# A fused transformer kernel on one core: the norms between its stages and the start of its down projections rewritten

## The chip, the cores and the metric

The kernel runs on one core of a Trainium2 chip. The core has a matmul engine (TensorE, PE in the profile; PEld are its weight loads), VectorE (DVE), ScalarE (ACT), GpSimd (POOL) and the queue engine SyncE (SP) that issues most DMAs. Each engine has its own instruction stream; they meet only at semaphores. The metric is the device time of one execution in microseconds (us), lower being better.

## The reference

One call computes a block with a gated recurrent mixer and a long convolution, and then two more layers. In order:

```python
# first block
u = rms_norm(x, mix_pre_g) * (1 + sc1) + sh1          # sh, sc, g come from cond @ ada_w
h, y = mlstm(u), conv_branch(u)
mix = concat([h, y]) @ w_out
x = x + g1 * rms_norm(mix, mix_post_g)
u = rms_norm(x, ffn_pre_g) * (1 + sc2) + sh2
a, gt = split(causal_dwconv(u @ ffn_up))
x = x + g2 * rms_norm((silu(gt) * a) @ ffn_down, ffn_post_g)
# two layers, mixer = attention with forget gates, then a gated linear recurrence
x = x + rmsnorm(mixer(rmsnorm(x, gain0)), gain1)
x = x + rmsnorm(swiglu_ffn(rmsnorm(x, gain2)), gain3)
```

x is 512 positions by 1024 channels, the feed-forward width is 2816, everything is float32.

## The kernel before

**Layout.** Activations lie channel-major: a tensor of 1024 channels is 8 tiles (KT = 8) of 128 partitions by 512 positions (T). x, m (the output of the last projection), u_hi and u_lo (the next stage's input, split into a rounded float32r part and the rest) live in SBUF. There are eight PSUM banks, ps[0] to ps[7], of 128x512 float32.

**Matmuls.** Each float32 product is three float32r matmuls of 512 columns (hi by hi, lo by hi, hi by lo), all recorded at line 308 (gemm_chunk), 332 (gemm_first) or 488 (the mixers' outputs). Weights stream from HBM in chunks of 128x1024. SP loads chunk c + 4 into the slot of chunk c once c has been used; POOL rounds it (w_hi, line 812) and takes the rest (w_lo, line 818); then PE may use it. That order is fixed: POOL goes through the chunks in the stream's order, with the sums of the norms (below) put in between.

**Up and down.** Each feed-forward stage makes 22 pairs of up chunks (FT = 22). The gate and the product of pair j are made by DVE and ACT into f_hi and f_lo, with banks 2s and 2s+1 for s = j % 2. Then out_pe makes the 8 output tiles of the down projection, each of three chunks of 8, 7 and 7 k-tiles, in banks 0 and 1 in turn. Before output tile n it waits for the copy of tile n - 2:

```python
pe.wait_ge(og.act.sem, og.act.at("copy", og_body * it + s - 2))
```

For the first two tiles there is no such copy: the semaphore has a credit of two turns, which og.act.open(act) adds. In the kernel before, that call is the first statement of out_act on ACT's stream, behind the last gate of the up stage. out_act then squares each output tile into sq and copies it into m, and DVE adds the squares into acc.

**Norms.** There are seven: n0 before the first mixer (no output tile before it), n1 before the first feed-forward stage ("shift", with a modulation), n2 to n5 ("late"), n6 at the end (only the residual). For each but n0: PE sums acc and the last square over the channels (line 345, 347), ACT takes Ln and Exp (lines 369, 371) to get 1/rms in ps[5], DVE makes t = m * gain / rms (line 431) and x = x + t (line 435), tile by tile. norm_act begins with an ACT table load (line 374).

In a late norm the next projection does not wait for the second rms: per tile ACT makes u_hi = x * gain (line 381) and the square (384), DVE makes u_lo (424), and gemm_first starts with tile 0 of three chunks at once. POOL adds up the squares (413, 416), late_sum_pe sums them over the channels behind gemm_first (359), and the projection's results are scaled by this second 1/rms (the tile rms) afterwards. While it waits for the first u_lo, PE runs six filler matmuls (keep_busy, line 339).

**Modulation.** The adaptive modulation columns are made in four turns of DVE partial products (ada_dve_pieces) and PE column sums (ada_pe, line 636) during the first mixer's output projection.

Of the kernel before, what the change touches and what calls it, by code (L numbers as in the profile page):

```python
# [18 lines left out]
P = 128  # L19
T = 512  # L20
D = 1024
KT = D // P
# [6 lines left out]
FT = 2816 // P  # L29
# [71 lines left out]
def build(nc, xT, wstream, ada, params, outT, rows1, rows2):  # L101
# [150 lines left out]
    class Norm:  # L252
# [3 lines left out]
        def __init__(self, name, post, pre):  # L256
            self.post, self.pre = post, pre
            if post:
# [3 lines left out]
                for n in range(KT):  # L262
                    order += [f"t{n}"] + ([f"lo{n - 1}"] if n and pre == "late" else []) + [f"x{n}"]
                self.vx = Steps(ctx, nc, name + "_dvex", order + ([f"lo{KT - 1}"] if pre == "late" else []))
# [7 lines left out]
            if pre == "late":  # L272
                self.ahq = Steps(ctx, nc, name + "_acthisq", [f"{w}{n}" for n in range(KT) for w in ("hi", "sq")])
# [4 lines left out]
    norms = [Norm(f"n{i}", i > 0, pre) for i, pre in enumerate(("shift", "shift", "late", "late", "late", "late", None))]  # L278
# [6 lines left out]
    outs = [OutGemm(f"og{i}") for i in range(6)]  # L285

# [49 lines left out]
    def keep_busy(pe, count):  # L336

        for _ in range(count):
            nc.tensor.matmul(ps[2][:], mean_w[:], levels[:, 0:4, :].bitcast(f32), start=True, stop=True)

    def norm_pe(pe, N, og):
        if N.post:
# [4 lines left out]
            N.pe1.did(nc.tensor.matmul(ps[5][:], mean_w[:], sq[(KT - 1) % 2][:], start=False, stop=True), "sum")  # L347
            if N.pre == "late":
                keep_busy(pe, 6)
        if N.pre == "shift":  # L350
# [3 lines left out]
            keep_busy(pe, 3)  # L354
# [18 lines left out]
    def norm_act(act, N, gain, shift):  # L373
        act.preload_act_table_set(LN_EXP)  # L374
# [3 lines left out]
        if N.pre == "late":  # L378
            for n in range(KT):
                act.wait_ge(N.vx.sem, N.vx.at(f"x{n}"))  # L380
                N.ahq.did(nc.scalar.activation(u_hi[:, n, :], x[:, n, :], ACT.Identity, scale=gain(n)), f"hi{n}")  # L381
                if n >= 2:
                    act.wait_ge(N.pq.sem, N.pq.at(f"add{max(n - 2, 1)}"))
                N.ahq.did(nc.scalar.activation(sq[n % 2][:], x[:, n, :], ACT.Square), f"sq{n}")
# [22 lines left out]
    def norm_pool(pool, N):  # L407

        if N.pre == "late":
# [9 lines left out]
    def norm_dve(dve, N, post_gain, gain, shift, wait_cols=None):  # L419

        def low_late(n):

            dve.wait_ge(N.ahq.sem, N.ahq.at(f"hi{n}"))
            N.vx.did(nc.vector.scalar_tensor_tensor(u_lo[:, n, :], x[:, n, :], gain(n), u_hi[:, n, :].bitcast(f32),  # L424
                                                    ALU.mult, ALU.subtract), f"lo{n}")

        if N.post:
            dve.wait_ge(N.a1.sem, N.a1.at("rstd"))
            for n in range(KT):
                t = ps[4 + 2 * (n % 2)]  # L430
# [1816 lines left out]
```

## Time and profile before

| | before |
|---|---|
| median of 3 runs | 2395.82 us (2394.5 to 2397.46) |
| the profiled execution's own time | 2394.99 us |
| its span, first to last instruction | 2393.2 us |
| PE busy | 2273.7 us, 95% |
| POOL busy | 1478.8 us, 62% |
| DVE busy | 1163.8 us, 49% |
| ACT busy | 629.0 us, 26% |
| mean granted TensorE clock | 0.979 |

Busy time says how long instructions of an engine were under way. A matmul is recorded as longer than its share of the engine, since matmuls overlap, so the distance between the starts of two of them is the measure of their pace.

### The profile page before, as it was taken

Reading aid. Unit: us, or ns where it says so; the run is one execution under the profiler, and the core shown is the slowest. Engines: PE = TensorE matmul, PEld = TensorE weight load, DVE = VectorE, ACT = ScalarE, POOL = GpSimd, SP = SyncE. Lnnn points to the kernel's source line nnn. Section 1 sums busy time; section 2 is a strip of 40 time slices with the busy share of each in tenths; the row PEclk is TensorE's granted clock in tenths of the full one; section 3 lists DMA queues with packets and bytes.
Section 4 is the critical chain, followed back from the end, with each engine's and each line's share of the span. In section 5 each row is a group of like instructions: output and inputs, shape, how many; then the busy total and the mean of one; then the engine's idle time right before and its main releaser. Section 6 shows DMA issues by size and latency. Waiting matters only on the chain. (4 is left out here: it accounts for less than half of the span.)

```text
span 2393.2 us, 28178 instructions
## 1 busy us (share of the span) xinstructions
PE 2273.7 (95%) x9952; PEld 1768.8 (74%) x9952; DVE 1163.8 (49%) x1942; ACT 629.0 (26%) x1077; POOL 1478.8 (62%) x704
## 2 busy tenths in 40 slices
PE   7999999999999998999899999998898979999997
PEld 4777776767887876777678887876777767888785
DVE  4878877974433007555342221027778755322112
ACT  2322325132222013333331111023444433111100
POOL 3756763648777886444288777884222228877784
PEclk9999999999999999999999999999999989999999
DMA  5322323722222331222122322321111112222232
GB/s 217 106 80 71 96 88 106 288 76 93 96 96 80 105 104 63 71 71 71 53 74 93 96 93 91 105 79 62 53 53 53 60 37 80 90 94 96 88 105 79
DMA packets 56503, 216.35 MB, mean 90 GB/s; under 512 B 6232, under 2 KB 6232, under 8 KB 53232
## 3 DMA queue, kind: packets, MB, share of 16 engines
q1 hardware_dynamic: 52992, 206.96, 25.9%
q10 hardware_dynamic: 3440, 8.44, 1.0%
q8 instruction: 45, 0.74, 0.1%
q14 instruction: 26, 0.21, 0.0%
HBM read 213.23 MB, written 2.15 MB: 90 GB/s over the span
## 5 line engine op out<-in xcount | busy, mean ns | idle before, releaser
L812 POOL TENSOR_TENSOR w_hi<-raw,ones 128x1024 fp32r<-128x1024 f32 x315 | 603.0, 1914 | 628.8 <-DMA raw<-in_wstream 627.7
L818 POOL TENSOR_TENSOR w_lo<-raw,w_hi 128x1024 fp32r<-128x1024 f32 x342 | 837.3, 2448 | 230.7 <-ACT w_hi L1521 206.0
L308 PE MATMUL ps<-u_hi,w_hi 128*128 128x512 f32 x1760 | 719.2, 409 | 13.1 <-DVE hv L1974 6.2
L308 PE MATMUL ps<-u_lo,w_hi 128*128 128x512 f32 x1760 | 699.3, 397 | 0.0
L308 PE MATMUL ps<-u_hi,w_lo 128*128 128x512 f32 x1760 | 698.5, 397 | 0.0
L308 PEld LDWEIGHTS ps<-u_hi,w_hi 128*128 128x128 f32 x1760 | 334.1, 190 | 92.1 <-issue 7.7
L308 PEld LDWEIGHTS ps<-u_hi,w_lo 128*128 128x128 f32 x1760 | 332.6, 189 | 81.4
L308 PEld LDWEIGHTS ps<-u_lo,w_hi 128*128 128x128 f32 x1760 | 333.7, 190 | 75.9 <-issue 3.1
L308 PE MATMUL ps<-f_hi,w_hi 128*128 128x512 f32 x528 | 210.5, 399 | 7.7 <-ACTq L85 7.7
L308 PE MATMUL ps<-f_hi,w_lo 128*128 128x512 f32 x528 | 210.1, 398 | 0.0
L308 PE MATMUL ps<-f_lo,w_hi 128*128 128x512 f32 x528 | 210.0, 398 | 0.0
L1668 DVE SCALAR_TENSOR_TENSOR y<-ps,prm,y 128x511 f32<-128x511 f32 (+14 forms) x240 | 176.1, 734 | 11.0 <-ACT y L1266 3.4
L529 DVE TENSOR_TENSOR acc<-acc,sq 128x512 f32<-128x512 f32 x30 | 39.8, 1326 | 253.0 <-ACT sq L519 252.8
L519 ACT ACTIVATE sq<-ps 128x512 f32<-128x512 f32 x48 | 28.7, 599 | 472.0 <-PE ps L308 350.7
L1934 DVE TENSOR_TENSOR ps<-ps,rms 128x512 f32<-128x512 f32 x44 | 30.7, 698 | 194.0 <-PE ps L308 194.0
L308 PEld LDWEIGHTS ps<-f_hi,w_hi 128*128 128x128 f32 x528 | 100.0, 189 | 33.2 <-issue 5.0
L308 PEld LDWEIGHTS ps<-f_hi,w_lo 128*128 128x128 f32 x528 | 99.9, 189 | 24.7
L308 PEld LDWEIGHTS ps<-f_lo,w_hi 128*128 128x128 f32 x528 | 100.0, 189 | 24.4
L1143 PE MATMUL ps<-hl 128*128 128x128 f32 x448 | 63.9, 288 | 30.3 <-DVE hl L2049 25.9
L1143 PEld LDWEIGHTS ps<-hl 128*128 128x128 f32 x448 | 61.2, 201 | 39.2 <-DVE hl L2049 30.2
L1484 ACT ACTIVATE f_hi<-fraw 128x512 f32 x44 | 27.8, 632 | 210.3 <-DVE fraw L1939 210.3
L1932 DVE TENSOR_TENSOR ps<-ps,rms 128x512 f32<-128x512 f32 x44 | 30.7, 698 | 94.0 <-PE ps L308 84.3
(305 smaller groups left out, 2928.5 us busy)
## 6 DMA issues: line engine op xcount, KB each, us to landing
raw<-in_wstream SPq DMA_DIRECT2D x342, 512.0 KB, 3.4
ada_buf<-in_ada SPq DMA_DIRECT2D x16, 1024.0 KB, 5.8
ada_start<-in_ada SPq DMA_DIRECT2D x8, 1024.0 KB, 16.7
cbc<-decay_rows ACTq DMA_DIRECT2D x8, 512.0 KB, 3.7
x<-in_xT SPq DMA_DIRECT2D x1, 2048.0 KB, 7.6
bc<-gate_rows ACTq DMA_DIRECT2D x4, 512.0 KB, 4.9
out_T<-x ACTq DMA_DIRECT2D x8, 256.0 KB, 2.0
prm<-in_params SPq DMA_DIRECT2D x1, 357.5 KB, 3.0
```

The source lines that it names most:

```text
L308: last = nc.tensor.matmul(out, a, b, start=(start and k == 0 and i == 0), stop=(stop and k == nk - 1 and i == 2))
L519: og.act.did(nc.scalar.activation(sq[n % 2][:], ps[n % banks][:], ACT.Square), "sq")
L529: ins = nc.vector.tensor_tensor(acc[:], acc[:], sq[n % 2][:], ALU.add)
L812: g.tensor_tensor(w_hi[slot][:], raw[slot][:], ones[:, 0:1].to_broadcast([P, D]), ALU.mult).then_inc(chunk_hi, 1)
L818: g.tensor_tensor(w_lo[slot][:], raw[slot][:], w_hi[slot][:].bitcast(f32), ALU.subtract).then_inc(chunk_split, 1)
L1143: last = nc.tensor.matmul(ps[b][:, ts], (hk if src is None else src)[:, ts], (hq if src is None else src)[:, ts], start=True, stop=True)
L1484: aS.did(A(f_hi[:, bass.ds(j, 1), :], fraw[s][:, 0:T], ACT.Identity), "hi")
L1668: v_cv[i].did(V.scalar_tensor_tensor(y[:, 2 * h + i, back:], ps[4 + i][:, 0:T - back], head_col(h, HP_CVW + CV_TAPS * i + j), y[:, 2 * h + ...
L1932: vS.did(V.tensor_tensor(ps[2 * s][:], ps[2 * s][:], rms[:], ALU.mult), "sg")
L1934: vS.did(V.tensor_tensor(ps[2 * s + 1][:], ps[2 * s + 1][:], rms[:], ALU.mult), "sa")
```

## The change

1. The credit of all six output projections is given at the very start of ACT's stream (open_outs). In place of the old wait, ffn_pe waits before the down projection for step "f" of pair FT - 2, the last pair that used banks 0 and 1.
2. The ACT table load for Ln and Exp moves from the start of norm_act to the start of out_act.
3. In n1, the last turn of the modulation is summed on PE behind the norm's own sum, into bank 3, and its columns are made on DVE behind the residual.
4. In n2 to n5, t and the new x are made in a PSUM bank out of three (4, 6 and 2 or 3). u_hi, u_lo and the square read it there, and ACT copies x back to SBUF: three ACT passes a tile instead of two. t of tile n waits for the square of tile n - 3. The filler matmuls write bank 7.
5. In n6, t of even tiles is made in place in m, and POOL adds it to x; DVE does the odd tiles as before.

```diff
--- before.py
+++ after.py
@@ -253,14 +253,17 @@
-        def __init__(self, name, post, pre):
-            self.post, self.pre = post, pre
+        def __init__(self, name, post, pre, spare):
+            self.post, self.pre, self.banks = post, pre, (4, 6, spare)
             if post:
                 self.pe1 = Steps(ctx, nc, name + "_pe1", ["sum"])
                 self.a1 = Steps(ctx, nc, name + "_act1", ["ln", "rstd"])
                 order = []
                 for n in range(KT):
                     order += [f"t{n}"] + ([f"lo{n - 1}"] if n and pre == "late" else []) + [f"x{n}"]
+                if pre is None:
+                    order = [step for n in range(KT) for step in ([f"t{n}", f"x{n}"] if n % 2 else [f"t{n}"])]
+                    self.px = Steps(ctx, nc, name + "_poolx", [f"x{n}" for n in range(0, KT, 2)])
                 self.vx = Steps(ctx, nc, name + "_dvex", order + ([f"lo{KT - 1}"] if pre == "late" else []))
             if pre == "shift":
                 self.asq = Steps(ctx, nc, name + "_actsq", ["sq"])
@@ -270,12 +273,17 @@
                 self.ah = Steps(ctx, nc, name + "_acthi", ["hi"])
                 self.vl = Steps(ctx, nc, name + "_dvelo", ["lo"])
             if pre == "late":
-                self.ahq = Steps(ctx, nc, name + "_acthisq", [f"{w}{n}" for n in range(KT) for w in ("hi", "sq")])
+                self.ahq = Steps(ctx, nc, name + "_acthisq", [step for n in range(KT + 1) for step in
+                                                        ([f"hi{n}"] if n < KT else []) + ([f"x{n - 1}", f"sq{n - 1}"] if n else [])])
                 self.pq = Steps(ctx, nc, name + "_poolsq", [f"add{n}" for n in range(1, KT)])
                 self.pe2 = Steps(ctx, nc, name + "_pe2", ["sum"])
                 self.a2 = Steps(ctx, nc, name + "_act2", ["ln", "rstd"])
-    norms = [Norm(f"n{i}", i > 0, pre) for i, pre in enumerate(("shift", "shift", "late", "late", "late", "late", None))]
+        def new(self, n):
+            return ps[self.banks[n % 3]]
+    norms = [Norm(f"n{i}", i > 0, pre, 2 if i == 2 else 3) for i, pre in enumerate(("shift", "shift", "late", "late", "late", "late", None))]
     class OutGemm:
         def __init__(self, name):
@@ -283,6 +291,10 @@
             self.dve = Steps(ctx, nc, name + "_dve", [f"acc{n}" for n in range(1, KT - 1)])
     outs = [OutGemm(f"og{i}") for i in range(6)]
+    def open_outs(act):
+        for og in outs:
+            og.act.open(act)
     def matmuls(out, pairs, n_inc=None, start=True, stop=True):
@@ -333,25 +345,27 @@
                 if k == KT - 1:
                     last.then_inc(gemm_done, 1)
-    def keep_busy(pe, count):
+    def keep_busy(pe, count, bank):
         for _ in range(count):
-            nc.tensor.matmul(ps[2][:], mean_w[:], levels[:, 0:4, :].bitcast(f32), start=True, stop=True)
-
-    def norm_pe(pe, N, og):
+            nc.tensor.matmul(ps[bank][:], mean_w[:], levels[:, 0:4, :].bitcast(f32), start=True, stop=True)
+    def norm_pe(pe, N, og, between=None):
         if N.post:
             pe.wait_ge(og.dve.sem, og.dve.at(f"acc{KT - 2}"))
             nc.tensor.matmul(ps[5][:], mean_w[:], acc[:], start=True, stop=False)
             pe.wait_ge(og.act.sem, og.act.at("sq", KT - 1))
             N.pe1.did(nc.tensor.matmul(ps[5][:], mean_w[:], sq[(KT - 1) % 2][:], start=False, stop=True), "sum")
+            if between:
+                between()
             if N.pre == "late":
-                keep_busy(pe, 6)
+                keep_busy(pe, 6, 7)
         if N.pre == "shift":
             for n in range(KT):
                 pe.wait_ge(N.asq.sem, N.asq.at("sq", n))
                 N.pe2.did(nc.tensor.matmul(ps[7][:], mean_w[:], sq[n % 2][:], start=(n == 0), stop=(n == KT - 1)), "sum")
-            keep_busy(pe, 3)
+            keep_busy(pe, 3, 2)
     def late_sum_pe(pe, N):
@@ -371,17 +385,26 @@
         S.did(nc.scalar.activation(out[:], out[:], ACT.Exp, scale=-0.5), "rstd")
     def norm_act(act, N, gain, shift):
-        act.preload_act_table_set(LN_EXP)
+        if not N.post:
+            act.preload_act_table_set(LN_EXP)
+        def late_home(n):
+            act.wait_ge(N.vx.sem, N.vx.at(f"lo{n}"))
+            N.ahq.did(nc.scalar.activation(x[:, n, :], N.new(n)[:], ACT.Identity), f"x{n}")
+            if n >= 2:
+                act.wait_ge(N.pq.sem, N.pq.at(f"add{max(n - 2, 1)}"))
+            N.ahq.did(nc.scalar.activation(sq[n % 2][:], N.new(n)[:], ACT.Square), f"sq{n}")
         if N.post:
             act.wait_ge(N.pe1.sem, N.pe1.at("sum"))
             inverse_root(act, N.a1, ps[5], ps[5], 1)
         if N.pre == "late":
             for n in range(KT):
                 act.wait_ge(N.vx.sem, N.vx.at(f"x{n}"))
-                N.ahq.did(nc.scalar.activation(u_hi[:, n, :], x[:, n, :], ACT.Identity, scale=gain(n)), f"hi{n}")
-                if n >= 2:
-                    act.wait_ge(N.pq.sem, N.pq.at(f"add{max(n - 2, 1)}"))
-                N.ahq.did(nc.scalar.activation(sq[n % 2][:], x[:, n, :], ACT.Square), f"sq{n}")
+                N.ahq.did(nc.scalar.activation(u_hi[:, n, :], N.new(n)[:], ACT.Identity, scale=gain(n)), f"hi{n}")
+                if n:
+                    late_home(n - 1)
+            late_home(KT - 1)
             act.wait_ge(N.pe2.sem, N.pe2.at("sum"))
             inverse_root(act, N.a2, rms, ps[7], 1)
         if N.pre == "shift":
@@ -406,6 +429,10 @@
     def norm_pool(pool, N):
+        if N.pre is None:
+            for n in range(0, KT, 2):
+                pool.wait_ge(N.vx.sem, N.vx.at(f"t{n}"))
+                N.px.did(nc.gpsimd.tensor_tensor(x[:, n, :], x[:, n, :], m[:, n, :], ALU.add), f"x{n}")
         if N.pre == "late":
             for n in range(1, KT):
                 pool.wait_ge(N.ahq.sem, N.ahq.at(f"sq{n}"))
@@ -418,21 +445,28 @@
     def norm_dve(dve, N, post_gain, gain, shift, wait_cols=None):
         def low_late(n):
             dve.wait_ge(N.ahq.sem, N.ahq.at(f"hi{n}"))
-            N.vx.did(nc.vector.scalar_tensor_tensor(u_lo[:, n, :], x[:, n, :], gain(n), u_hi[:, n, :].bitcast(f32),
-                                                    ALU.mult, ALU.subtract), f"lo{n}")
+            N.vx.did(nc.vector.scalar_tensor_tensor(u_lo[:, n, :], N.new(n)[:], gain(n),
+                                                    u_hi[:, n, :].bitcast(f32), ALU.mult, ALU.subtract), f"lo{n}")
         if N.post:
             dve.wait_ge(N.a1.sem, N.a1.at("rstd"))
             for n in range(KT):
-                t = ps[4 + 2 * (n % 2)]
-                N.vx.did(nc.vector.scalar_tensor_tensor(t[:], m[:, n, :], post_gain(n), ps[5][:], ALU.mult, ALU.mult), f"t{n}")
+                t = N.new(n)[:] if N.pre == "late" else ps[4 + 2 * ((n if N.pre else n // 2) % 2)][:]
+                if N.pre is None and n % 2 == 0:
+                    t = m[:, n, :]
+                if N.pre == "late" and n >= 3:
+                    dve.wait_ge(N.ahq.sem, N.ahq.at(f"sq{n - 3}"))
+                N.vx.did(nc.vector.scalar_tensor_tensor(t, m[:, n, :], post_gain(n), ps[5][:], ALU.mult, ALU.mult), f"t{n}")
                 if n and N.pre == "late":
                     low_late(n - 1)
+                if N.pre is None and n % 2 == 0:
+                    continue
                 dve.wait_ge(N.vx.sem, N.vx.at(f"t{n}"))
-                N.vx.did(nc.vector.tensor_tensor(x[:, n, :], x[:, n, :], t[:], ALU.add), f"x{n}")
+                N.vx.did(nc.vector.tensor_tensor(t if N.pre == "late" else x[:, n, :], x[:, n, :], t, ALU.add), f"x{n}")
             if N.pre == "late":
                 low_late(KT - 1)
         if N.pre == "shift":
@@ -511,7 +545,7 @@
     def out_act(act, og, base, ks, banks=2, done=None):
         nch = len(ks)
-        og.act.open(act)
+        act.preload_act_table_set(LN_EXP)
         for n in range(KT):
             act.wait_ge(gemm_done, done(n) if done else base + (n + 1) * nch)
             if n >= 2:
@@ -618,10 +652,12 @@
     ada_link = Steps(ctx, nc, "ada_link", [f"l{s}{k}" for s in range(ADA_BODY) for k in range(KT - 1)])
+    ADA_BANK = (6, 6, 6, 3)
     def ada_dve_mod(dve, turn):
         dve.wait_ge(p_ada.sem, p_ada.at("sums", turn))
         n = ADA_BODY * ADA_COLS // P
-        v_mod.did(nc.vector.tensor_tensor(mod[:, 2 * KT + n * turn:2 * KT + n * (turn + 1)], ps[6][:, 0:n],
+        v_mod.did(nc.vector.tensor_tensor(mod[:, 2 * KT + n * turn:2 * KT + n * (turn + 1)], ps[ADA_BANK[turn]][:, 0:n],
                                           prm[:, COL["ada_b"] + 2 * KT + n * turn:COL["ada_b"] + 2 * KT + n * (turn + 1)],
                                           ALU.add), "mod")
@@ -988,7 +1024,7 @@
             pe.wait_ge(outs[0].act.sem, outs[0].act.at("copy", n - GROUP))
             wout_pe(n, 0, range(KT))
             wout_pe(n, 1, range(KT))
-            turn = {3: 0, 5: 1, 6: 2, 7: 3}.get(n)
+            turn = {3: 0, 5: 1, 6: 2}.get(n)
             if turn is not None:
                 ada_pe(pe, turn)
@@ -1012,10 +1048,11 @@
                     for j in range(2):
                         pair(it, s, j)
             S, step = prev
+            pe.wait_ge(S.sem, S.at("f", FT - 2))
             out_pe(pe, og, dbase, DOWN_K, lambda k: f_hi[:, k, :], lambda k: f_lo[:, k, :],
                    ready=lambda k: pe.wait_ge(S.sem, S.at(step, k)))
-        norm_pe(pe, norms[1], outs[0])
+        norm_pe(pe, norms[1], outs[0], lambda: ada_pe(pe, 3))
         ffn_pe(norms[1], C_UP1, C_DOWN1, {"g": (v_ff1, "g0"), "a": (v_ff1, "a0")}, outs[1], (v_ff1, "lo"))
         norm_pe(pe, norms[2], outs[1])
@@ -1229,6 +1266,7 @@
     @block.scalar
     def _(act):
         A = nc.scalar.activation
+        open_outs(act)
         act.wait_ge(prm_landed, 16)
         a_set.did(A(cvec[:], prm[:, COL["c"]:COL["c"] + KT], ACT.Sigmoid), "sig_c")
         act.wait_ge(const_ready, 14)
@@ -1595,7 +1633,8 @@
         out_act(act, outs[5], C_DOWN3, DOWN_K)
         norm_act(act, norms[6], None, None)
         for n in range(KT):
-            act.wait_ge(norms[6].vx.sem, norms[6].vx.at(f"x{n}"))
+            S = norms[6].vx if n % 2 else norms[6].px
+            act.wait_ge(S.sem, S.at(f"x{n}"))
             act.dma_start(outT[:, n, :], x[:, n, :]).then_inc(out_landed, 16)
         act.wait_ge(out_landed, 16 * KT)
@@ -1780,18 +1819,27 @@
             for n in (2 * it, 2 * it + 1):
                 if 1 <= n < KT - 1:
                     out_sum_dve(dve, outs[0], n)
-        ada_dve_mod(dve, KT // 2 - 1)
-        dve.wait_ge(v_mod.sem, v_mod.at("mod", KT // 2 - 1))
-        for name, o, src, gain in (("g1", 8, 16, "mix_post"), ("a2", 16, 32, "ffn_pre"), ("g2", 24, 40, "ffn_post")):
...
-        dve.wait_ge(v_col.sem, v_col.at("g2"))
+        def modulation_columns(names):
+            for name, o, src, gain in (("g1", 8, 16, "mix_post"), ("a2", 16, 32, "ffn_pre"), ("g2", 24, 40, "ffn_post")):
+                if name in names:
...
+            dve.wait_ge(v_col.sem, v_col.at(names[-1]))
+        def last_columns():
+            ada_dve_mod(dve, KT // 2 - 1)
+            dve.wait_ge(v_mod.sem, v_mod.at("mod", KT // 2 - 1))
+            modulation_columns(["g2"])
+        dve.wait_ge(v_mod.sem, v_mod.at("mod", KT // 2 - 2))
+        modulation_columns(["g1", "a2"])
         norm_dve(dve, norms[1], lambda n: col_a[:, 8 + n:9 + n], lambda n: col_a[:, 16 + n:17 + n],
-                 lambda n: mod[:, 24 + n:25 + n])
+                 lambda n: mod[:, 24 + n:25 + n], last_columns)
         v_ff1.open(dve)
```

## Rows read from the trace of the kernel before

**Rows 1.** The page, part 1: busy time, share of span, instructions of each engine.
```profile
PE 2273.7 (95%) x9952; PEld 1768.8 (74%) x9952; DVE 1163.8 (49%) x1942; ACT 629.0 (26%) x1077; POOL 1478.8 (62%) x704
```

**Rows 2.** Waits of PE, whole span: total us, times, longest us.
```profile
PE ps L308 <- ACTq L85: 7.7, 3, 3.4
```

**Rows 3.** Timeline of PE at two down projections: start us, us, instruction.
```profile
768.80 0.77 PE L308 MATMUL ps<-f_hi,w_hi 128*128 128x512 f32 x1 [3.44 <-ACTq L85]
...
774.06 0.44 PE L308 MATMUL ps<-f_hi,w_hi 128*128 128x512 f32 x1
...
2248.33 0.39 PE L308 MATMUL ps<-u_hi,w_lo 128*128 128x512 f32 x1
2250.83 0.47 PE L308 MATMUL ps<-f_hi,w_hi 128*128 128x512 f32 x1 [2.11 <-ACTq L85]
```

**Rows 4.** Windows: PE, PEld, DVE, ACT, POOL busy (count), PEclk, DMA.
```profile
2250.80:2256.00 5.20, 5.17 (x16) 4.13 (x17) 0.69 (x1) 0.25 (x1) 3.92 (x3) 0.67 0.16 66
...
2250.00:2376.00 126.00, 125.17 (x529) 100.40 (x530) 11.67 (x8) 8.41 (x16) 92.63 (x43) 0.99 0.27 87
```

**Rows 5.** Timeline of the start of n1.
```profile
495.38 1.84 PE L636 MATMUL ps<-ones,ada_acc 128*128 128x1 f32 x16
...
499.08 0.66 ACT L369 ACTIVATE ps<-ps,eps_col 128x512 f32<-128x512 f32 x1 [1.12 <-PE ps L347]
```

**Rows 6.** Timeline of n6, all engines.
```profile
2375.63 1.02 PE L345 MATMUL ps<-acc,mean_w 128*128 128x512 f32 x2
...
2376.49 1.12 PE L347 MATMUL ps<-sq,mean_w 128*128 128x512 f32 x2
2376.93 1.28 ACT L374 ACT_TABLE_LOAD   x1
...
2379.54 0.76 DVE L431 SCALAR_TENSOR_TENSOR ps<-m,prm,ps 128x512 f32<-128x512 f32 x1 [15.65 <-ACT ps L371]
...
2381.05 0.37 ACTq L1599 DMA_DIRECT2D out_T<-x  x1
...
2390.04 0.69 DVE L435 TENSOR_TENSOR x<-x,ps 128x512 f32<-128x512 f32 x1
```

**Rows 7.** Timeline of n5, a late norm, all engines.
```profile
1994.25 5.31 PE L339 MATMUL ps<-levels,mean_w 128*128 128x512 f32 x12
...
1996.34 0.76 DVE L431 SCALAR_TENSOR_TENSOR ps<-m,prm,ps 128x512 f32<-128x512 f32 x1 [7.70 <-ACT ps L371]
...
1999.70 0.47 PE L332 MATMUL ps<-u_hi,w_hi 128*128 128x512 f32 x1
...
2013.01 0.68 DVE L435 TENSOR_TENSOR x<-x,ps 128x512 f32<-128x512 f32 x1
...
2015.05 1.33 POOL L416 TENSOR_TENSOR acc<-acc,sq 128x512 f32<-128x512 f32 x1 [0.82 <-ACT sq L384]
...
2017.49 1.02 PE L359 MATMUL ps<-acc,mean_w 128*128 128x512 f32 x2
...
2024.45 0.50 PE L308 MATMUL ps<-u_hi,w_hi 128*128 128x512 f32 x1 [0.34 <-POOL w_lo L818]
```

**Rows 8.** Timeline of n2, the late norm behind the first down projection.
```profile
898.39 0.76 DVE L431 SCALAR_TENSOR_TENSOR ps<-m,col_a,ps 128x512 f32<-128x512 f32 x1 [17.77 <-ACT ps L371]
...
920.42 1.02 PE L359 MATMUL ps<-acc,mean_w 128*128 128x512 f32 x2
```

**Rows 9.** Lines: count, ns min/median/max, first to last start.
```profile
L405 ACT ACTIVATE u_hi<-ps,mod x16: 687/687/691, 43.8 to 525.1; 128x512 fp32r<-128x512 f32 x16
...
L520 ACT ACTIVATE m<-ps x48: 590/592/620, 420.2 to 2376.3; 128x512 f32<-128x512 f32 x48
...
L424 DVE SCALAR_TENSOR_TENSOR u_lo<-x,prm,u_hi x32: 750/752/2497, 900.7 to 2014.5; 128x512 fp32r<-128x512 f32 x32
...
L435 DVE TENSOR_TENSOR x<-x,ps x48: 673/682/687, 501.2 to 2390.0; 128x512 f32<-128x512 f32 x48
```

**Rows 10.** One line of the last mixer's recurrence, columns as in rows 9.
```profile
L2083 DVE TENSOR_TENSOR hqd<-hq,he x8: 675/2882/2901, 1665.7 to 1942.4; 128x512 f32<-128x512 f32 x8
```

More of the change, by code:

```diff
@@ L635, in ada_pe @@
                 j = s * (ADA_COLS // P) + h
-                last = nc.tensor.matmul(ps[6][:, j:j + 1], ada_acc[:, 4 * (turn % 2) + s, h * P:(h + 1) * P], ones[:, 0:1],
+                last = nc.tensor.matmul(ps[ADA_BANK[turn]][:, j:j + 1], ada_acc[:, 4 * (turn % 2) + s, h * P:(h + 1) * P], ones[:, 0:1],
                                         start=True, stop=True)
@@ L1782, in _ @@
                     out_sum_dve(dve, outs[0], n)
-        ada_dve_mod(dve, KT // 2 - 1)
-        dve.wait_ge(v_mod.sem, v_mod.at("mod", KT // 2 - 1))
-        for name, o, src, gain in (("g1", 8, 16, "mix_post"), ("a2", 16, 32, "ffn_pre"), ("g2", 24, 40, "ffn_post")):
-            g_ = prm[:, COL[gain]:COL[gain] + KT]
-            if name == "a2":
-                ins = V.scalar_tensor_tensor(col_a[:, o:o + KT], mod[:, src:src + KT], 1.0, g_, ALU.add, ALU.mult)
-            else:
-                ins = V.tensor_tensor(col_a[:, o:o + KT], mod[:, src:src + KT], g_, ALU.mult)
-            v_col.did(ins, name)
-        dve.wait_ge(v_col.sem, v_col.at("g2"))
+        def modulation_columns(names):
+            for name, o, src, gain in (("g1", 8, 16, "mix_post"), ("a2", 16, 32, "ffn_pre"), ("g2", 24, 40, "ffn_post")):
+                if name in names:
+                    g_ = prm[:, COL[gain]:COL[gain] + KT]
+                    if name == "a2":
+                        ins = V.scalar_tensor_tensor(col_a[:, o:o + KT], mod[:, src:src + KT], 1.0, g_, ALU.add, ALU.mult)
+                    else:
+                        ins = V.tensor_tensor(col_a[:, o:o + KT], mod[:, src:src + KT], g_, ALU.mult)
+                    v_col.did(ins, name)
+            dve.wait_ge(v_col.sem, v_col.at(names[-1]))
[5 more added lines that the diff above has]
+        modulation_columns(["g1", "a2"])
         norm_dve(dve, norms[1], lambda n: col_a[:, 8 + n:9 + n], lambda n: col_a[:, 16 + n:17 + n],
-                 lambda n: mod[:, 24 + n:25 + n])
+                 lambda n: mod[:, 24 + n:25 + n], last_columns)
         v_ff1.open(dve)
```

## The prediction

> **What bounds the kernel now.** The page's first part comes first: PE is busy for 95% of the span, the other engines for 62% at most [rows 1]. So PE is the bound, and a change gains where it removes time in which PE waits or runs slowly, or shortens the end behind its last matmul. The pace of PE at full clock is one matmul in 0.233 us (two starts in a row in the timeline, such as 2375.63 less the start before it). I then looked for PE's waits. One is met at all three down projections: together 7.7 us, put down to ACT's queue [rows 2]. The timelines show it as a hole between the last up matmul and the first down matmul, and behind it matmuls at a wider distance [rows 3]; a window gives the granted clock there, 0.67 [rows 4]. The rest of PE's idle time lies mostly in the norms, so I read one late norm in order of time [rows 7], another for the difference [rows 8], and the last one [rows 6].
>
> **The credits given at the start.** The last up matmul of the third feed-forward stage starts at 2248.33, the first down matmul at 2250.83; at full pace it would follow after 0.23, so 2.27 us are lost. The profile's idle of 2.11 is this less 0.16, since it counts from the modelled end. For three holes: 7.7 + 3 x 0.16 = 8.2 us [rows 2, 3]. What PE would then wait for is old: step "f" of pair 20 comes two chunks, some 11 us, before. The last gate's own tile is wanted 21 k-tiles on, 63 x 0.233 = 14.7 us later, and it follows the last up matmul by about 3 us. Weights: POOL is busy for 92.6 of 126 us in the down stage [rows 4], and PE waits for nothing else there.
>
> The hole costs more than itself. At 768.80 the matmuls start at wide distances until 774.06: 12 matmuls in 5.26 us, at full pace 2.80, so 2.46 us more. Behind the third hole there are 16 matmuls in 5.2 us at a granted clock of 0.67, where 3.73 would do: 1.47 more [rows 3, 4]. These stretches are at the lower of TensorE's two levels, 1.2 GHz, and follow a PE that stood still. With no hole I take both to go. Bounds: 0 (the slow stretch comes anyway) to 3.9 us. I take 3.9, as PE runs at full clock up to each hole. **Sum: 8.2 + 3.9 = 12.1 us.**
>
> **The table load.** In n6 the norm's sum ends at 2376.49 + 1.12 = 2377.61 but Ln starts only behind the table load, 2376.93 + 1.28 = 2378.21. Ln moves forward to 2377.65, by 0.57, in n2 to n6 [rows 6]. In its new place the load lies in ACT's wait for the first output tile. The Trainium skill ("ScalarE: Activation LUTs", What ACT_TABLE_LOAD costs) gives 1283 ns and a further 1380 ns of drain for a switch to another set. The trace has only the 1.28; by the page each norm would give 1.4 more, 8 us in all, and the rows leave no room for it.
>
> **n1.** Here the column sums of the modulation stand ahead: 495.38 is where the norm's first sum would start. In n6 Ln could start 2377.65 - 2375.63 = 2.02 behind that point; here it starts at 499.08 instead of 497.40. **Gain 1.7 us** [rows 5, 6]. The moved PE work (1.84 us) lies before the first square of the new x, and its DVE columns lie in the wait for the second 1/rms.
>
> **The late norms.** Let t0 be the first t, 0.57 earlier than now. Per tile the chain is x 0.68, u_hi 0.69 (the ACT form that reads PSUM with a column), then u_lo, from which the next x follows 0.67 later, with two hand-overs of 0.03: 2.11 us, hardly less than now [rows 7, 9]. But u_lo now reads x and u_hi, both in SBUF, and takes up to 2497 ns instead of 752, while x, with one operand in PSUM, never took over 687 in 48 cases [rows 9]. I take POOL's work on SBUF operands as what holds it up. With x in PSUM, u_lo reads one SBUF operand, and I take 0.75 each time. The Trainium skill ("SBUF — State Buffer", Who interferes with whom) says the same: a VectorE instruction with two SBUF inputs and a GpSimd one that reads SBUF exclude each other, and the first to start keeps the other out. By it the remaining two-operand work of the recurrence stays exposed, and a shift in time decides anew who is blocked; that is the last rival.
>
> The last x then ends at t0 + 0.79 + 0.68 + 7 x 2.11 = t0 + 16.2 (now t0 + 17.35). Against this stands ACT's third pass. Behind the last x come u_hi 0.69, the copy 0.59 and the square of tile 6, 0.60, then two POOL sums of 1.33 one behind the other, so late_sum_pe starts at t0 + 20.9 [rows 7, 9]. Now it starts behind gemm_first, at t0 + 21.15 in n5 and t0 + 22.03 in n2 [rows 7, 8]. In n2, and in n4 that also follows a down projection, the mixer waits for what hangs on this sum: gain 22.03 - 20.9 + 0.57 = 1.7 each. In n5 and n3 the next chunk of weights counts too. The filler matmuls keep PE until 1994.25 + 12 x 0.43 = 1999.4, so gemm_first starts 0.3 earlier than now, and without pauses (72 x 0.233 = 16.8) ends at 2016.2 instead of 2017.49. The weights would allow 2016.2 + 6.96 = 2023.16; PE, held by the sum at 1995.77 + 20.9 and 6.62 us of work, comes to 2023.3, instead of 2024.45: gain 1.15 each [rows 7]. **Together 5.7 us.** No row has an addition in place in PSUM; nearest is line 435 at 0.68, and I take that. Bounds for four norms: 0 (ACT's passes hold t back through the ring of three banks) to 9 (PSUM passes overlap by 0.1 each and POOL's sums hide).
>
> **n6.** Eight pairs of t and x now take 2390.04 + 0.69 - 2379.54 = 11.19 us, 1.39 a pair: t 0.78 with its wait, x 0.61. New, for two tiles: 0.67 (t with no wait behind it) + 0.78 + 0.61 = 2.06; four times, with the last x to its end, 8.3 us. POOL's last sum starts behind t6 at 6.9 and ends at 8.3 as well. So 2.9 less, but the two last outputs are issued one behind the other on ACT, 0.37 each [rows 6], and share the DMA engines, which I put at 0.4 (bounds 0 and 1.4, the present distance of two outputs). With the table load, 0.57: **2.7 us**, bounds 1.7 and 3.5.
>
> **The sum.** 12.1 + 1.7 + 5.7 + 2.7 = 22.2 us. The profiled execution took 2394.99 us, 1.8 beyond its span, and becomes 2372.8. The median lies 0.8 above it: 2395.82 - 22.2 = **2373.6 us**.
>
> **Rivals.**
> - *The late norms give nothing.* ACT's third pass delays the squares, POOL's sums and t of tile n + 3 until what u_lo gains is eaten. For: 20.9 against 21.15 is close, and one more late ACT pass of 0.6 would do. Against: ACT needs 1.9 us of the 2.11 a tile. Time: 2373.6 + 5.7 = 2379.3. Chance 0.15.
> - *The slow clock stays.* The low level behind the holes moves elsewhere in the stage. Time: 2377.5. Chance 0.1.
> - *The credits do nothing.* PE at the down projection waits for weights or for the new step instead. Against: POOL is free for a quarter of that stage. Time: 2373.6 + 12.1 = 2385.7. Chance 0.03.
> - *Slower: the recurrence is re-timed badly.* Behind n4 PE waits for DVE, whose operations with two SBUF operands are blocked by POOL: line 2083 takes 2882 ns in the middle case and 675 at best [rows 10]. One more blocked one costs 2.2 us, and there are 8 turns. Two more in each turn cost 35 us: 2408.8. It decides from about 10 more, or 1.3 a turn. Against: some are blocked already, and a shift should free as many as it hits. Chance 0.03.
> - My forecast: 0.69, with its own range 2368 to 2378.
>
> The whole range takes in the first two rivals and a few collisions either way: 2367 to 2381. A measurement tells 0.2% (4.8 us) from no change. Faster by more: all but the last rival and little beside it, 0.95; same 0.02; slower 0.03.
>
> **What would show it.** Down projections: the first matmul 0.23 us behind the last up matmul, full clock behind it, about 4 us from the cold stretches. Norms: Ln right behind the sum; no u_lo over 0.8 us; late_sum_pe later behind gemm_first than now, by 0.5 us. n6: last x 8.3 us behind the first t. I am wrong if PE has a new wait at the late sum of over 1 us, if the clock falls in stretches where it is full now, or if the recurrence between 1640 and 1960 us changes its length by more than 3 us.

## The result and the profile after

The changed kernel takes 2373.6 us in the median (2370.2 to 2375.2, 4 runs), beside 2396.6 for the kernel before: the medians are 23.1 us apart, and the ratio is put at 0.9899 with a 95% interval of 0.9887 to 0.9912. A second measurement of the same pair gave 0.9904 (0.9889 to 0.9919). The forecast was 2373.6 us and 22.2 us less. The profiled execution has a span of 2370.6 us, 22.6 less than before.

The page's first part, as in [rows 1]: PE is busy 8 us less with the same 9952 matmuls, since slow matmuls are recorded as longer; ACT has 32 instructions more, the copies of x.

```profile
span 2370.6 us, 28211 instructions
PE 2265.5 (96%) x9952; PEld 1766.9 (75%) x9952; DVE 1147.8 (48%) x1938; ACT 642.3 (27%) x1109; POOL 1483.7 (63%) x708
```

Waits of PE over the span. The wait of [rows 2] is gone, and no new one takes its place at the down projections. Gone too is the wait of gemm_first for the late norms' u_lo, of which the first line here shows the one before; the rest is from the changed kernel. Two lines are new: PE waits once, for 1.2 us, for the copy of an output tile in the mixers' outputs (the same loop, line 488 before, had 1.1 us behind POOL's w_lo), and it waits for POOL's sums ahead of the four late sums, 0.2 us each. The long waits of the mixers, such as the first of the changed kernel's lines, are as they were.

```profile
PE ps L332 <- DVE u_lo L424: 4.7, 5, 1.7
```

```profile
PE ps L1180 <- DVE hl L2097: 26.0, 9, 5.7
...
PE ps L320 <- POOL w_lo L854: 4.8, 2, 3.5
...
PE ps L522 <- ACT m L554: 1.2, 1, 1.2
PE ps L373 <- POOL acc L443: 0.8, 4, 0.2
```

The timeline of PE at the first and the third down projection, against [rows 3]: the first matmul on f_hi starts 0.23 us behind the last on u_hi, and the next ones keep that pace.

```profile
765.17 0.39 PE L320 MATMUL ps<-u_hi,w_lo 128*128 128x512 f32 x1
765.40 0.40 PE L320 MATMUL ps<-f_hi,w_hi 128*128 128x512 f32 x1
765.63 0.39 PE L320 MATMUL ps<-f_lo,w_hi 128*128 128x512 f32 x1
...
2232.49 0.40 PE L320 MATMUL ps<-u_hi,w_lo 128*128 128x512 f32 x1
2232.72 0.39 PE L320 MATMUL ps<-f_hi,w_hi 128*128 128x512 f32 x1
```

Windows of the third down stage, against [rows 4], with the same columns: 24 matmuls in 5.2 us where there were 16, at a granted clock of 1.00.

```profile
2232.50:2237.70 5.20, 5.20 (x24) 4.19 (x23) 2.09 (x3) 1.92 (x2) 3.97 (x3) 1.00 0.33 101
2232.50:2355.90 123.40, 123.40 (x530) 99.15 (x529) 6.24 (x9) 9.53 (x16) 95.87 (x44) 1.00 0.28 89
```

n1, against [rows 5]: the norm's sum comes first, the modulation's column sums follow, and Ln starts 2.01 us behind the first sum (499.16 less 497.15), where it started 3.70 us behind the same point.

```profile
497.15 1.02 PE L357 MATMUL ps<-acc,mean_w 128*128 128x512 f32 x2
...
498.96 1.73 PE L672 MATMUL ps<-ones,ada_acc 128*128 128x1 f32 x15
499.16 0.66 ACT L383 ACTIVATE ps<-ps,eps_col 128x512 f32<-128x512 f32 x1 [0.73 <-PE ps L359]
```

n2: the late sum (line 373) is 20.80 us behind the first t of 891.92, where it was 22.03 [rows 8]. The u_lo are no longer held up. First the two rows of the kernel before: its first u_lo started 0.40 us behind POOL's w_lo and took 2.50, until 0.55 behind the end of that w_lo.

```profile
900.26 2.35 POOL L818 TENSOR_TENSOR w_lo<-raw,w_hi 128x1024 fp32r<-128x1024 f32 x1
...
900.66 2.50 DVE L424 SCALAR_TENSOR_TENSOR u_lo<-x,prm,u_hi 128x512 fp32r<-128x512 f32 x1
```

In the changed kernel the first u_lo (line 452) begins while POOL's w_hi (line 848) is under way, and w_lo starts in the midst of it; it takes 0.75 us. The whole trace says it more plainly. Of the 32 u_lo before, six began inside an operation of POOL, and these six are the ones that took 0.94 to 2.50 us; the other 26 took 0.75. Now 28 of the 32 begin inside one, and none takes more than 0.753.

```profile
891.92 0.75 DVE L463 SCALAR_TENSOR_TENSOR ps<-m,col_a,ps 128x512 f32<-128x512 f32 x1 [17.20 <-ACT ps L385]
...
894.16 0.75 DVE L452 SCALAR_TENSOR_TENSOR u_lo<-ps,prm,u_hi 128x512 fp32r<-128x512 f32 x1
...
894.38 2.38 POOL L854 TENSOR_TENSOR w_lo<-raw,w_hi 128x1024 fp32r<-128x1024 f32 x1
...
909.94 2.73 POOL L443 TENSOR_TENSOR acc<-acc,sq 128x512 f32<-128x512 f32 x2 [0.83 <-ACT sq L396]
...
912.72 1.12 PE L373 MATMUL ps<-acc,mean_w 128*128 128x512 f32 x2 [0.20 <-POOL acc L443]
```

n6, against [rows 6]: Ln starts right behind the sum's end at 2357.90, and the last x ends 8.28 us behind the start of the first t, where it was 11.19. POOL's last x (line 435) ends at 2367.48, within 0.04 us of DVE's.

```profile
2356.78 1.12 PE L359 MATMUL ps<-sq,mean_w 128*128 128x512 f32 x2
2357.94 0.66 ACT L383 ACTIVATE ps<-ps,eps_col 128x512 f32<-128x512 f32 x1 [0.73 <-PE ps L359]
...
2359.24 0.75 DVE L463 SCALAR_TENSOR_TENSOR m<-m,prm,ps 128x512 f32<-128x512 f32 x1 [17.20 <-ACT ps L385]
...
2366.21 1.27 POOL L435 TENSOR_TENSOR x<-x,m 128x512 f32<-128x512 f32 x1 [0.78 <-DVE m L463]
2366.83 0.69 DVE L469 TENSOR_TENSOR x<-x,ps 128x512 f32<-128x512 f32 x1
```

**Where the time went, stage by stage.** PE's timeline has marks that every kernel shares: the first sum of each norm, each late sum, the first matmul of each down projection. The distances between them, in us, for the two profiled executions (the distances to the end of the span are known to a tenth only):

| from, to | before | after | less |
|---|---|---|---|
| start, end of the first mixer (n1's sum, or the column sums ahead of it) | 495.38 | 497.15 | -1.77 |
| that point, first up matmul | 21.86 | 20.25 | 1.61 |
| first up stage, to its down projection | 251.56 | 248.00 | 3.56 |
| first down stage | 125.69 | 123.20 | 2.49 |
| n2, sum to late sum | 25.93 | 24.12 | 1.81 |
| late sum to the first logits | 14.40 | 14.15 | 0.25 |
| attention mixer | 281.07 | 281.09 | -0.02 |
| n3, sum to late sum | 25.46 | 24.13 | 1.33 |
| late sum to down projection | 233.35 | 230.70 | 2.65 |
| second down stage | 123.27 | 123.20 | 0.07 |
| n4, sum to late sum | 25.92 | 24.13 | 1.79 |
| late sum to the recurrence | 15.49 | 15.25 | 0.24 |
| recurrence | 353.06 | 352.28 | 0.78 |
| n5, sum to late sum | 25.05 | 24.12 | 0.93 |
| late sum to down projection | 233.34 | 230.95 | 2.39 |
| third down stage | 124.80 | 123.21 | 1.59 |
| n6, to the end of the span | 17.57 | 14.67 | 2.90 |
| whole span | 2393.2 | 2370.6 | 22.6 |

The first row is no effect of the change. The mark where the first mixer's output projection begins, ahead of every stage that the change shortens, lies at 394.0 us in the execution before, at 396.5 here, and between 394.0 and 399.7 in all kernels below. The recurrence takes 351.9 to 354.8 us in them. The changed kernel's two profiled executions, with spans of 2370.6 and 2375.7 us, differ by 3.2 us in that start-up and by 2.5 in the recurrence, which is why the experiments are read by these distances more than by their time.

### The profile page after: what moved, and what is told of

It is laid out like the page before. It is cut to its first block and busy times, and to the rows that moved or that the text cites. A ratio compares the mean times of both kernels' runs of the same rounds, so it can differ in the third digit from the quotient of the medians.

```text
span 2370.6 us, 28211 instructions
## 1 busy us (share of the span) xinstructions
PE 2265.5 (96%) x9952; PEld 1766.9 (75%) x9952; DVE 1147.8 (48%) x1938; ACT 642.3 (27%) x1109; POOL 1483.7 (63%) x708
## 5 line engine op out<-in xcount | busy, mean ns | idle before, releaser
L563 DVE TENSOR_TENSOR acc<-acc,sq 128x512 f32<-128x512 f32 x30 | 31.9, 1062 | 256.5 <-ACT sq L553 256.2
```

The source lines that it names most:

```text
L563: ins = nc.vector.tensor_tensor(acc[:], acc[:], sq[n % 2][:], ALU.add)
```

## The experiments

**1. The credits alone.** The kernel before, with

```diff
+        open_outs(act)                                  # start of ACT's stream
...
-        og.act.open(act)                                # in out_act
...
+            pe.wait_ge(S.sem, S.at("f", FT - 2))        # ahead of out_pe
```

> The kernel before with the credits at the start and the new wait for step f, and nothing else of the change. Theory (the holes and the slow clock behind two of them both go): 12.1 us less, 8.2 for the three holes and 3.9 for the slow stretches; first down matmul 0.23 us behind the last up matmul at each stage, granted clock 1.00 behind it. Rival (the slow stretch comes anyway, somewhere in the down stage): 8.2 us less, and windows of 5 us in the down stages still show a clock near 0.5 or 0.7.

Measured: 2387.15 us against 2397.8, ratio 0.9954 (0.9940 to 0.9968), 11 us less with an interval of 8 to 14. The time alone does not part the two theories. The trace does: the down stages take 123.20 us in all three places, as in the changed kernel, so nothing of the slow clock is left. The three holes are gone as well: the stages ahead of the down projections are 3.75, 2.19 and 2.30 us shorter. With the 4.2 of the slow stretches that is 12.4 us by the traces, where the theory had 12.1.

**2. The holes kept but filled.** The kernel before, with these lines ahead of out_pe. The old wait stays where it was, behind them, so that PE runs the fillers and then waits for what is left of the hole:

```diff
+            pe.wait_ge(S.sem, S.at("f", FT - 2))
+            for _ in range(4 if base == C_UP1 else 2):
+                nc.tensor.matmul(ps[0][:], mean_w[:], levels[:, 0:4, :].bitcast(f32), start=True, stop=True)
```

> The kernel before, its holes kept, but PE runs filler matmuls in them (four of 0.86 us at the first down projection, two at the others), so that it does not stand still. Theory (the slow clock follows from PE standing still in the hole): the holes stay as long, the clock behind them is 1.00, and the down stages become shorter by 2.5 us in the first and 1.5 in the third, about 3.9 us less in all. Rival (the clock falls for another reason, the work being the same): the slow stretches stay and the time is that of before, or a little longer.

Measured: 2395.19 us against 2397.8, ratio 0.9988 (0.9979 to 0.9997). The first up stage is as long as before (251.42), so the hole is there, and the down stages take 123.28, 123.27 and 123.28 us. Their sum is 3.9 us less than in the execution before. Windows across the first and the third hole show full clock:

```profile
762.00:782.00 20.00, 20.00 (x79) 14.55 (x79) 4.45 (x6) 2.10 (x4) 12.52 (x7) 1.00 0.24 79
2245.00:2265.00 20.00, 19.61 (x82) 14.84 (x81) 2.08 (x3) 0.63 (x1) 13.31 (x7) 1.00 0.29 103
```

So the slow matmuls behind a hole come from PE's standing still: the hole is as long here, and only PE's activity in it differs. They are worth 1.4 to 2.5 us where they come. They do not always come, so the third hole of one execution would prove little by itself; the first hole is the better witness, since it is followed by them in all four executions that leave it empty. The next experiment leaves the holes alone, and its third down stage takes 123.27 us and its first 124.62; the windows show 1.00 and 0.91 there:

```profile
2245.00:2265.00 20.00, 17.89 (x77) 14.12 (x77) 2.08 (x3) 2.29 (x3) 14.35 (x7) 1.00 0.24 80
762.00:782.00 20.00, 16.56 (x66) 12.99 (x65) 4.44 (x6) 3.15 (x4) 11.18 (x6) 0.91 0.24 79
```

**3. The table load alone.** The kernel before, with

```diff
+        if not N.post:                                  # start of norm_act
             act.preload_act_table_set(LN_EXP)
...
+        act.preload_act_table_set(LN_EXP)               # in out_act, ahead of the tiles
```

> The kernel before with the table load moved ahead of the output tiles, and nothing else. Theory: Ln starts 0.04 us behind the end of the norm's sum, 0.57 us earlier than before, in n2 to n6; 2.9 us less in all. In n3 and n5, where the filler matmuls end 0.3 us before gemm_first starts, only 0.3 us of it can reach PE, which makes it 2.3. Rival (the load only moves the wait, since something else of ACT is drained with it): nothing, 0 us.

Measured: 2394.58 us against 2397.8, ratio 0.9987 (0.9976 to 0.9998), in line with the sum. But each norm disagrees with my even share of 0.57. From sum to late sum: n2 24.29 (1.64 less), n3 25.47 (nothing), n4 24.25 (1.67 less), n5 25.31 (0.26 more); n6 0.59 less. POOL and DVE of n2 show why: the first u_lo, which starts 5.59 us behind the norm's sum instead of 6.17, is now ahead of the w_lo of the last chunk and takes 0.77. This w_lo then takes 2.72 us where it had 2.35, and the second u_lo is held up instead, for 1.41.

```profile
900.81 2.72 POOL L820 TENSOR_TENSOR w_lo<-raw,w_hi 128x1024 fp32r<-128x1024 f32 x1
...
900.51 0.77 DVE L425 SCALAR_TENSOR_TENSOR u_lo<-x,prm,u_hi 128x512 fp32r<-128x512 f32 x1
...
902.67 1.41 DVE L425 SCALAR_TENSOR_TENSOR u_lo<-x,prm,u_hi 128x512 fp32r<-128x512 f32 x1
```

In n3 and n5 the first u_lo now starts 0.5 and 0.6 us behind the beginning of POOL's w_hi, where it had been 1.1 and 1.5, and so meets more of it: it takes 1.95 and 1.80 us, where the kernel before had 1.36 and 0.94. With x in SBUF, what the earlier Ln is worth is a matter of how it falls among POOL's operations.

**4. The sums ahead of the last weight split.** The kernel before, with

```diff
+            hold = 1 if N.pre == "late" else 0
-            split_range(at, end)
+            split_range(at, end - hold)
             norm_pool(pool, N)
-            at = end
+            at = end - hold
```

> The kernel before, but in n2 to n5 POOL makes the sums of the squares before it splits the last of the four chunks of weights, so that POOL touches nothing in SBUF while DVE makes the first u_lo. u_lo still reads x and u_hi, both in SBUF. Theory (the long u_lo were held up by POOL's work on SBUF): every u_lo takes about 0.75 us, those of 1.4 and 2.5 are gone; the late split is paid afterwards, PE waits for that chunk some 2 to 3 us in each late norm. Rival (the first u_lo is slow by itself, because x in SBUF has just been written, or by the start of gemm_first): 0.9 to 2.5 us as before.

Measured: one time, 2398.5 us, which by itself says nothing. All 32 u_lo take 750 to 755 ns, with both operands in SBUF as before; only POOL's turn at the weights has moved behind them. Against line 424 in [rows 9]:

```profile
L424 DVE SCALAR_TENSOR_TENSOR u_lo<-x,prm,u_hi x32: 750/752/755, 900.9 to 2016.0; 128x512 fp32r<-128x512 f32 x32
```

The price is there too: from the late sum to the down projection 235.25 and 236.81 us, 1.9 and 3.5 more, as PE waits for the late chunk. That shows that it was POOL that held up u_lo, and not the operand having just been written. From sum to late sum the four norms take 24.18 or 24.19 us here, although the table load is still in its old place. That is 0.5 less than experiment 5 finds for x in PSUM with the table load there. Behind the last u_lo the late sum follows after 2.25 us here and after 3.03 there, with ACT's third pass in between. So x in PSUM is not free either; what it saves over this kernel is the wait for the late chunk.

**The changed kernel again.** It ran beside the kernels of experiments 5 to 7, on the same chip as they did.

> The changed kernel once more, on the same chip as the three variants of it, to compare them with. Every theory: about 23 us less than before.

Measured: 2374.6 us against 2398.35, ratio 0.9904 (0.9889 to 0.9919). The recurrence took 354.79 us in this profiled execution and 352.28 in the first.

**5. The table load put back in the changed kernel.** The edit is the opposite of experiment 3's.

> The changed kernel with the table load back at the start of norm_act. Theory (with x in PSUM no u_lo is held up, whenever it starts): every u_lo 0.75 us; from a late norm's sum to its late sum 24.13 + 0.57 = 24.7 us in all four, against 24.13 in the changed kernel, 25.9, 25.5, 25.9, 25.05 in the one before and 24.3, 25.5, 24.25, 25.3 with the load moved alone; Ln of n6 0.57 later. So 2.9 us more than the changed kernel. Rival (the earlier start is what keeps the first u_lo away from POOL's weight split, and PSUM gives nothing): u_lo of 2.5 us come back in n2 and n4, and the kernel is 6 to 7 us longer than the changed one.

Measured: 2376.67 us against 2398.35, ratio 0.9917 (0.9904 to 0.9931), where the changed kernel had 0.9904 on the same chip. From sum to late sum 24.70 us in all four norms, as forecast, and every u_lo is 750 to 753 ns:

```profile
L451 DVE SCALAR_TENSOR_TENSOR u_lo<-ps,prm,u_hi x32: 750/751/753, 898.5 to 2006.0; 128x512 fp32r<-128x512 f32 x32
```

In n2 the first u_lo meets POOL as in the kernel before: w_lo starts at 898.22 and u_lo 0.31 us behind it, and it takes 0.752 us where it took 2.497. That is the operand's place alone, at the same meeting. n6 takes 15.30 us instead of 14.67 to 14.74. With experiment 3 all four combinations of the two parts have been run. From sum to late sum, in us:

| | n2 | n3 | n4 | n5 |
|---|---|---|---|---|
| before | 25.93 | 25.46 | 25.92 | 25.05 |
| table load moved | 24.29 | 25.47 | 24.25 | 25.31 |
| x in PSUM | 24.70 | 24.69 | 24.70 | 24.70 |
| both (changed kernel) | 24.12 | 24.13 | 24.13 | 24.12 |

The two parts are not additive in n2 and n4 (1.2 and 1.6 alone, 1.8 together) since either one takes the first u_lo out of POOL's way. In n3 and n5 only x in PSUM does.

**6. PE kept busy ahead of the two later mixers.** The changed kernel, with

```diff
         fox_gemm(0)
+        pe.wait_ge(norms[2].a2.sem, norms[2].a2.at("ln"))
+        keep_busy(pe, 8, 7)
...
+        pe.wait_ge(norms[4].a2.sem, norms[4].a2.at("ln"))
+        keep_busy(pe, 6, 7)
         pe.wait_ge(v_hg0.sem, v_hg0.at("v"))
```

> The changed kernel with filler matmuls where PE stands still before the attention mixer (7.4 us, eight fillers) and before the recurrence (5.8 us, six fillers), behind which the profile shows a clock of 0.74 and 0.77 in the 20 us windows. Theory (what the holes of the down projections showed holds here: PE stands still, the clock falls, the matmuls behind it are slower): clock 1.00 there and up to 2.5 us less at each place. Rival (PE is not the bound at the start of the mixers, DVE and ACT are): the clock is 1.00 and the stages take as long as they did, 0 us.

Measured: 2371.68 us, ratio 0.9897 (0.9882 to 0.9912), beside 0.9904 for the changed kernel: not to be told apart. The clock theory holds, the gain does not follow. The windows of the changed kernel (first) and of this one (second) ahead of the attention mixer:

```profile
915.00:940.00 25.00, 17.58 (x71) 12.89 (x70) 16.80 (x32) 7.53 (x19) 18.05 (x8) 0.80 0.26 93
```

```profile
915.00:940.00 25.00, 23.72 (x100) 15.30 (x98) 18.39 (x37) 8.76 (x23) 16.94 (x8) 1.00 0.28 88
```

The attention mixer takes 280.65 us (280.5 and 281.1 in the changed kernel's two executions), so PE's clock at its start does not set its pace; that DVE and ACT do is the rival's reading, and was not tried by itself. Ahead of the recurrence the clock is full too, 1.00 from 1613 to 1627 us, where the changed kernel had 0.51 from 1619 to 1626, and the way there from n4's late sum is shorter, 14.00 us instead of 15.25. But then PE waits 6.4 us inside the recurrence, and the clock falls to 0.57 from 1627 to 1635; the recurrence takes 354.02 us, within what it takes elsewhere.

**7. The last outputs on two queues.** The changed kernel, with the DMAs of even tiles issued at the end of SP's stream instead of ACT's.

```diff
+        for n in range(0, KT, 2):
+            sp_.wait_ge(norms[6].px.sem, norms[6].px.at(f"x{n}"))
+            sp_.dma_start(outT[:, n, :], x[:, n, :]).then_inc(out_landed, 16)
...
+            if n % 2:                                       # in ACT's loop: the odd tiles only
```

> The changed kernel with the outputs of the even tiles issued by SP instead of ACT. Theory (the last two outputs lose 0.37 us of issue one behind the other): from the last x to the end of the span 2.7 us instead of 3.1, 0.4 us less. Rival (they lose it in the DMA engines that they share): 3.1 us as before. In the time of the whole kernel neither can be told; the end of the trace is what counts.

Measured: 2373.12 us, ratio 0.9901 (0.9886 to 0.9917); the stage from n6's sum to the end is 14.67 us, as with one queue. The last two outputs are issued at 2367.51 and 2367.55 us, where the changed kernel had 2367.51 and 2367.89, and yet the span ends 3.09 us behind the last x, as it did with one queue (3.11) and not as before (2.46). So the 0.6 us that the end takes longer than before is not issue time. The rival, that the outputs share the DMA engines, is what is left; no run tried it.

**8. The norms without the credits.** The edit is the opposite of experiment 1's, in the changed kernel.

> The changed kernel with the credits given where the kernel before gives them, behind the last gate. Theory (the parts add up, holes and slow clock belong to the credits alone): the three holes are back at 2.3 to 3.6 us, and the time lies 11 us below before: 1.6 for n1, 6.9 for the late norms, 2.9 for n6. Rival (part of what the late norms gain in n2 and n4 comes from the earlier end of the down projections): n2 and n4 take longer from their sum to the late sum than 24.13 us, and less than 9 us are left.

Measured: 2388.99 us against 2397.77, ratio 0.9966 (0.9953 to 0.9978), 8.2 us less with an interval of 5.3 to 11.3; 11 was at its edge. The norms are all there: 24.13 to 24.15 us from sum to late sum in all four, 14.71 for n6. The rival falls. What is different is the clock behind the holes. This execution has slow stretches behind all three, and down stages of 125.73, 124.82 and 124.73 us, 5.7 in all over 123.20, where the execution before had 4.2. By the traces the two halves of the change add up: 12.4 us for the credits in experiment 1 and 11.2 for the norms here (n1 1.6, the late norms 6.7, n6 2.9) make the 23.6 of the whole change. By the times they make 19 us of 23 to 24, which is at the edge of the three intervals. The window behind the second hole:

```profile
1463.00:1485.00 22.00, 19.89 (x79) 15.64 (x78) 2.79 (x4) 2.51 (x3) 14.12 (x7) 0.92 0.21 72
```

**9 and 10. Five filler matmuls, and none.** keep_busy(pe, 6, 7) in norm_pe of the changed kernel becomes keep_busy(pe, 5, 7), or is left out.

> The changed kernel with five filler matmuls in place of six in the late norms. Theory (six fillers end 0.12 us behind the moment at which the first u_lo would let PE start, and POOL's sums set the late sum anyway): gemm_first starts 6.44 us behind the norm's sum instead of 6.56, the late sum at 24.13 as before; the weights' path of n3 and n5 gains 0.1. Rival (with PE idle for 0.7 us ahead of gemm_first its clock falls): gemm_first takes longer by some us.

> The changed kernel with no filler matmuls in the late norms, so that PE stands still for some 5.4 us ahead of gemm_first. Theory (the holes showed it: PE that stands still is slow afterwards): gemm_first starts at 6.44 us but runs part of its 72 matmuls at 0.43 us each, the late sum comes 1.5 to 3 us later than at 24.13, in all four norms. Rival (the pace of DVE hides it, as 2.11 us a tile is nearly what PE needs): less than 0.5 us later.

Measured: 2372.5 and 2377.0 us, one time each. With five, gemm_first starts 6.45 us behind the norm's sum instead of 6.56 and the late sum comes at 24.12, so PE's start is no bound; the clock stays full in all four norms, against the rival. With none it starts at 6.46 and the late sum comes at 25.33, 25.53, 24.88 and 24.86, that is 0.7 to 1.4 us later: more than my rival, less than the 1.5 of the theory's low end. At n2 the first ten matmuls of gemm_first are some 0.43 us apart, the rest 0.23. Windows of ten us at n2, changed kernel and no fillers:

```profile
895.00:905.00 10.00, 10.00 (x43) 7.80 (x42) 9.51 (x15) 7.66 (x14) 5.64 (x4) 1.00 0.00 1
```

```profile
895.00:905.00 10.00, 9.74 (x33) 7.78 (x34) 9.51 (x16) 7.46 (x14) 5.79 (x4) 0.77 0.01 2
```

## Why the prediction was right, and where its steps were off

**The holes (8.2).** This was right: 3.56 + 2.27 + 2.27 = 8.1 us, taking the two later ones by their own starts. PE waits for nothing else there.

**The slow clock (3.9).** The mechanism is shown by experiments 1 and 2, and the stage table has 4.1 us for it. The size was one execution's, though. Sums of the down stages over 123.20 us each: 4.2 in the execution before, 1.5 and 1.6 in experiments 3 and 4, 5.7 in experiment 8. Their mean is 3.2, so the term could have come out anywhere from 1.5 to 5.7. My bounds, 0 to 3.9, took the one trace as the upper end, which it is not.

**n1 (1.7).** This was right: the trace has 1.61 us.

**The late norms (5.7).** The traces have 5.86 us up to the late sums, and 0.25 + 0.38 + 0.24 + 0.12 behind them, 6.9 in all. The chain came out as worked out: from the first t to the late sum 20.80 us for a forecast of 20.9. The reason that I gave, POOL holding up an operation with two SBUF operands, is shown by experiment 4, and that x in PSUM ends it by experiment 5. Two terms were mis-sized. I treated n3 like n5, though its first u_lo took 1.36 us and not 0.94: 1.15 forecast, 1.71 measured. In n2 and n4 the mixer started another 0.25 earlier, behind the late sum: 1.7 forecast, 2.05 measured. I also put the stall of PE at the late sum at about 0.5 us; by the starts of the matmuls it is 0.36, and 0.2 of that is a wait for POOL in the profile.

**The table load (0.57 a norm).** Right for n6 (0.59) and right on top of x in PSUM (24.70 to 24.13). As a part by itself it is wrong: alone it gave 1.6, 0, 1.7 and -0.3 us in n2 to n5, because it decides which operation of POOL a u_lo meets. My sum came out since it applied both. The 1.4 us of drain that the Trainium skill adds ("ScalarE: Activation LUTs", What ACT_TABLE_LOAD costs) did not show: the load put back costs 0.57 to 0.6 in each norm of experiment 5.

**n6 (2.7).** The trace has 2.9 us. The last x came at 8.28 us, as worked out. The tail behind it grew from 2.5 to 3.1, 0.6 instead of the 0.8 that I allowed, and experiment 7 shows that the issue, one half of that allowance, is not part of it.

**Rivals.** The late norms giving nothing: refuted, ACT's third pass fits between (PE waits 0.8 us for the sums in all). The credits doing nothing, and the slow clock staying: refuted by experiments 1 and 2. The badly re-timed recurrence: it took 351.9 to 354.8 us in the profiled executions of all kernels here, with 2.5 us between two executions of the changed kernel alone, so a loss of 20 us came in none of them.

**The sum.** 8.1 + 4.1 + 1.6 + 6.9 + 2.9 = 23.6 us by the traces, plus 0.8 in the recurrence and minus 1.8 at the start, gives the 22.6 between the two spans. That the forecast met the median to a tenth is luck: late norms and n6 were short by 1.4, the slow clock's term could have been 2 us smaller or larger, and the start-up moves by more than either.

Three things stay open: why a hole is followed by slow matmuls in one execution and not in the next, why the first mixer's output projection begins at 394 us in one execution and at 400 in another (the changed kernel alone has 396.5 and 399.7), and what lengthens the end behind the last x by 0.6 us. None of them was tried further.

## What to carry to other kernels

Where the bound engine stands still, read what it does in the microseconds behind the gap as well as the gap: here they added 1.5 to 5.7 us to 8.1 us of gaps, depending on the execution, so that one trace gives no upper bound. Where a DVE operation now and then takes two or three times its usual duration, look at which of its operands lie in SBUF and what POOL runs beside it; then either an operand in PSUM or POOL's work in another place ends it, and a change of time alone only moves it to the next operation. Where two parts of a change cure the same collision, run all four combinations (neither, each alone, both), since their gains do not add up.

## What the runs showed of the hardware

PE idle for 2.1 us by the profile was followed by a slow stretch in three of eight cases (second and third holes of four executions), and PE idle for 3.4 us in four of four (the first hole). Behind the third hole of [rows 3] the slow matmuls did not start at once: the first five were at full pace, then came about eight at 0.43 us apart.

The same operation of DVE took 752 ns in the middle case and up to 2497 ns at worst with both operands in SBUF (2610 in experiment 2), long only where it began inside an operation of POOL. With one operand in PSUM it took 753 ns at most in the changed kernel's first execution, 28 times of 32 beside a running operation of POOL. Where DVE began first, POOL's w_lo was the longer one, 2.72 us instead of 2.35 (experiment 3).
